# A hybrid transformer layer on one core: two small loads on ScalarE's queue, and a reordered last pair of experts

## The reference, cut to what matters

```python
h = LN(x)                                        # gain ln_in_g, offset ln_in_b
u = h @ w_in                                     # 115 tiles of 128 columns
m = sum_i sigmoid(gate_i) * (branch_i(u) @ wo_i) # gated linear attention, RWKV-7, Mamba-2
h = LN(alpha * h + m @ w_out)
# mixture of experts: 64 experts of width 256, 8 per token, and one shared expert
y = sum_e gate_e * ((silu(h @ w1_e) * (h @ w3_e)) @ w2_e) + shared(h)
out = LN(alpha * h + y)
```

## Time and profile before

| | |
|---|---|
| timed runs (3) | 1514.79, 1517.59, 1517.62 us, median 1517.59 |
| the profiled execution's own time | 1515.74 us |
| its span | 1513.9 us |
| TensorE busy | 1475.3 us, 97% |
| VectorE busy | 644.6 us, 43% |
| ScalarE busy | 389.7 us, 26% |
| GpSimd busy | 112.1 us, 7% |
| moved by the DMA engines | 371.36 MB |

### The profile page before, as it was taken

How to read it: one execution, slowest core, us unless ns; L and a number is a source line. 1 busy time by engine, 2 the same in 40 slices (tenths; PEclk the granted TensorE clock), 3 DMA queues, 4 the chain that set the end, 5 groups by cost and what they waited for, 6 DMA issues and landing times.

```text
span 1513.9 us, 31413 instructions
## 1 busy us (share of the span) xinstructions
PE 1475.3 (97%) x13271; PEld 1046.2 (69%) x13271; DVE 644.6 (43%) x1202; ACT 389.7 (26%) x873; POOL 112.1 (7%) x102
## 2 busy tenths in 40 slices
PE   7999999999999999999999999999999999999995
PEld 6676677777776777677667756777777777777751
DVE  5223787875635777634531133421121121111228
ACT  2112444443223544335421002011111111111111
POOL 4000113122010000000000000000000000000000
PEclk9999999999999999999999999999999999999998
DMA  7777375563345445563677548599999999999965
GB/s 236 166 178 170 111 213 168 135 203 104 108 116 159 112 115 139 193 191 110 195 235 225 148 166 362 195 400 409 417 411 405 415 413 401 418 412 405 411 269 172
DMA packets 155946, 371.36 MB, mean 245 GB/s; under 512 B 101596, under 2 KB 110188, under 8 KB 138144
## 3 DMA queue, kind: packets, MB, share of 16 engines
q1 hardware_dynamic: 123536, 340.11, 64.2%
q10 hardware_dynamic: 26416, 15.41, 3.4%
q0 software_dynamic: 5856, 13.85, 2.7%
HBM read 324.52 MB, written 50.64 MB: 248 GB/s over the span
## 4 chain that ended last, share of the span: by engine, by line
PE 83%; DVE 9%; DMA 2%; DVEq 2%; ACT 1%; issue 1%; ACTq 1%; SPq 0%
PE PS L563 25%; PE PS L1056 14%; PE PS L906 9%; PE PS L1023 8%; PE PS L1075 7%; PE PS L611 3%; DVE region L1455 2%; DVE region L1448 2%; PE PS L1028 2%; PE PS L944 2%; PE PS L1039 1%; ACT L1134 1%; PE PS L1064 1%; PE PS L619 1%; PE PS L804 1%
## 5 line engine op out<-in xcount | busy, mean ns | idle before, releaser
L563 PE MATMUL PS<-h0T,region 128*128 128x320 f32 x1808 | 510.4, 437 | 0.9 <-issue 0.8
L563 PEld LDWEIGHTS PS<-h0T,region 128*128 128x128 f32 x1808 | 336.9, 190 | 144.5 <-issue 12.2
L1134 ACT ACTIVATE region<-PS 128x9 f32<-128x9 f32 (+6 forms) x407 | 148.5, 383 | 686.6 <-PE PS L563 309.8
L1056 PE MATMUL PS<-region 128*64 128x512 f32 x1024 | 229.3, 592 | 0.0
L1056 PEld LDWEIGHTS PS<-region 128*64 128x64 f32 x1024 | 135.9, 137 | 83.3 <-issue 9.1
L1448 DVE TENSOR_TENSOR region<-region 128x256 f32<-128x256 f32 (+10 forms) x210 | 126.3, 621 | 96.1 <-ACTq L1177 75.5
L906 PE MATMUL PS<-region 128*128 128x320 f32 x512 | 138.3, 433 | 1.3 <-DMA region<-wo 1.2
L1023 PEld LDWEIGHTS PS<-region,h 128*128 128x128 f32 x1024 | 119.2, 192 | 26.4 <-issue 26.3
L1023 PE MATMUL PS<-region,h 128*128 128x128 f32 x1024 | 128.1, 278 | 0.3 <-issue 0.3
L906 PEld LDWEIGHTS PS<-region 128*128 128x128 f32 x512 | 97.0, 190 | 42.2 <-issue 1.9
L1075 PE MATMUL PS<-region,history 128*64 128x512 f32 x512 | 120.3, 596 | 0.5 <-ACTq L1413 0.5
(11 more groups left out here) (194 smaller groups left out, 1150.3 us busy)
## 6 DMA issues: line engine op xcount, KB each, us to landing
region<-moe_w SPq DMA_DIRECT2D x64, 2048.0 KB, 12.3
region<-moe_w SPq DMA_DIRECT2D x64, 1024.0 KB, 10.0
region<-w_in SPq DMA_DIRECT2D x115, 512.0 KB, 5.6
region<-wo SPq DMA_DIRECT2D x32, 512.0 KB, 3.8
projected<-region ACTq DMA_DIRECT2D x65, 167.5 KB, 3.9
expert_rows<-region SPq DMA_DIRECT2D x20, 512.0 KB
region<-expert_rows SPq DMA_DIRECT2D x4, 2048.0 KB, 12.6
region<-projected SPq DMA_DIRECT2D x10, 768.0 KB, 6.3
```

Source lines behind the costliest of these rows:

```text
L563: last = mm(PS[:, 6 + i % 2, 0:NTOK], WR[:, i, k, :], H0T[:, k, :], start=(k == 0), stop=(k == KT - 1))
L1056: last = mm(PS[tiles(i), 2, :], XE[:, k, tiles(i)], W13[r][i][:, k * 512:k * 512 + 512], start=(k == 0), stop=(k == KT - 1))
L1134: return nc.scalar.activation(out, in_, f, **kw)
```

## The change

Three things. (1) The loads of `ID` and `GBR` are started by ScalarE, first in its list, and no longer by SyncE between the first and the second token tile. (2) VectorE's list around the last two pairs is changed: the first addition of load 0 (`halve_rows(0)`) is put ahead of `x_step` of the last pair; the first of the two index comparisons is made one pair earlier; the rest of load 0's sum and all of load 1's follow the second comparison; the left copy of `Y` of the pair before last leaves VectorE. (3) ScalarE makes that left copy, behind its right copy and behind the start of one of the two loads of line 529, the one into partitions 64 to 127, which SyncE no longer starts. ScalarE first waits for `rows_out`, so that all scattered rows are in the table.

```diff
+        last_rows = slots[2048:SLOTS, :].rearrange("(p k) d -> p k d", k=8)
-        def sum_rows(e, k):
+        def sum_rows(e, k, halved=False):
             t, w = k // 2, 128 if k < 4 else 64
             rw = ROWS[k][0:w]
-            e.tensor_tensor(rw[:, 0:2], rw[:, 0:2], rw[:, 2:4], ALU.add)
-            e.drain()
+            if not halved:
+                e.tensor_tensor(rw[:, 0:2], rw[:, 0:2], rw[:, 2:4], ALU.add)
+                e.drain()
...
             sp.dma_start(H0[:, 0, :], x[:, 0, :]).then_inc(sem("x_first"), 16)
-            sp.dma_start(ID, io['consts'][:, C_ID:C_ID + 128]).then_inc(sem("ident_in"), 16)
-            sp.dma_start(GBR, io['lnv'][0:2, :].rearrange("r (k f) -> (r k) f", f=128)).then_inc(sem("ident_in"), 16)
             sp.dma_start(H0[:, 1, :], x[:, 1, :]).then_inc(sem("x_rest"), 16)
...
-            rows = slots[2048:SLOTS, :].rearrange("(p k) d -> p k d", k=8)
-            for h in range(2):
-                sp.dma_start(head(ROWS[4], h), rows[:, 4 * h:4 * h + 4, :]).then_inc(sem("halves_in"), 16)
+            sp.dma_start(head(ROWS[4], 0), last_rows[:, 0:4, :]).then_inc(sem("halves_in"), 16)
...
+            act.dma_start(ID, io['consts'][:, C_ID:C_ID + 128]).then_inc(sem("ident_in"), 16)
+            act.dma_start(GBR, io['lnv'][0:2, :].rearrange("r (k f) -> (r k) f", f=128)).then_inc(sem("ident_in"), 16)
...
                 act.wait_ge(sem("rows_out"), n + 1)
                 a_(Y[:, p, 512:D], PS[:, 6, :], ACT.Copy, scale=GA[:, p:p + 1])
                 act.drain().then_inc(sem("y_right"), 1)
+                if isinstance(n, int) and n == NP - 2:
+                    act.wait_ge(sem("rows_out"), SENT + 2)
+                    act.dma_start(head(ROWS[4], 1), last_rows[:, 4:8, :]).then_inc(sem("halves_in"), 16)
+                    a_(Y[:, p, 0:512], PS[:, 5, :], ACT.Copy, scale=GA[:, p:p + 1])
+                    act.drain().then_inc(sem("y_left"), 1)
...
+            def halve_rows(k):
+                dve.wait_ge(sem(f"rows_in{k}"), 16)
+                tt(ROWS[k][:, 0:2], ROWS[k][:, 0:2], ROWS[k][:, 2:4], add)
+                dve.drain()
...
+            def turned_back(p):
+                ts(OH[:, p].rearrange("p a b -> p (a b)")[:, 0:NTOK], CON[:, C_IOTA:C_IOTA + NTOK], TKI[:, p:p + 1],
+                   None, ALU.is_equal)
+                dve.drain().then_inc(sem("turned_back"), 1)
...
             for n in range(NP):
                 hid_step(n)
+                if n == NP - 2:
+                    halve_rows(0)
                 if n + 1 < NP:
                     x_step(n + 1, (n + 1) % 2, n + 1 < SENT)
                 if n + 2 < NP:
                     onehot(n + 2, n % 2, 0)
+                if n == NP - 3:
+                    turned_back(0)
                 if n == NP - 2:
-                    for p in range(2):
-                        ts(OH[:, p].rearrange("p a b -> p (a b)")[:, 0:NTOK], CON[:, C_IOTA:C_IOTA + NTOK], TKI[:, p:p + 1],
-                           None, ALU.is_equal)
-                        dve.drain().then_inc(sem("turned_back"), 1)
-                    add_rows(0)
+                    turned_back(1)
+                    sum_rows(dve, 0, True)
+                    add_rows(1)
                 if n == NP - 1:
                     add_rows(2)
-                y_step(n, n % 2)
-                if n == NP - 2:
-                    add_rows(1)
+                if n != NP - 2:
+                    y_step(n, n % 2)
             add_rows(3)
```

## The result

The changed kernel is slower. Eight runs of it have the median 1522.99 us (1519.95 to 1524.79), eight of the kernel before 1517.51 us; the ratio is 1.0036, 95% interval 1.0026 to 1.0045, which is 4 to 7 us. The forecast was 1516.6 and no measurable change.

A forecast was written before the change was run, and what follows sets the result against it. The wait chain runs over TensorE for 83% of the span, so only its exits at start and end count. Start -0.9 plus end +0.8 gives -0.1 us; from the middle of profiled and median times, 1516.6 us, range 1514.0 to 1519.2.

The forecast's parts named there:

- Step 1: First 14 us: small loads leave SyncE's queue, the second token tile's load is issued earlier; -0.9 us, at most 1.20.
- Step 2: VectorE's list before the last pair: 4.1 us of work gone, last pair's product earlier, 2.2 us won.
- Step 3: Last left copy of Y: at most 0.3 of 2.2 us reach the end, 1.9 become a wait for TensorE.
- Step 4: ScalarE after the pair before last: half load's issue and left copy finish before 1477, nobody waits; price nothing.
- Step 5: Half load on another queue delays load 3's landing to 1490.8; sum of load 3 +0.8 us, ends -0.3 and +2.7.
- R1: Load 3 pushed fully by the upper half load, landing at 1492.7 or 1493; +1.9 us net, 1517.6; chance 0.18.
- R2: Both edits harmless, loads 2 and 3 land in time; end gains 0.3, start 0.9: -1.2 us, 1514.5; chance 0.22.
- R3: Start gives nothing, small loads issued behind ScalarE's table load; start 0 to +0.3, end +0.8: +1.0, 1516.7; chance 0.11.
- R4: All VectorE saving reaches the end, needing the last down product before 1487; -3.1 us, 1512.6; chance 0.04.

The follow-up runs named there:

- the halves on SyncE: The changed kernel with both half loads back on SyncE's queue behind load 3; 1518.24 us, ratio 1.0005 to the kernel before.
- Filling that wait: Changed kernel, last tokens' rows in one wide SyncE load, load 3's first pass ahead of the last left copy of Y; 1514.78 us, ratio 0.9986 to before.
- the wide load on ScalarE's queue: Changed kernel, but ScalarE starts the last tokens' rows as one load over 128 partitions, SyncE only loads 0 to 3; 1518.17 us, one run.

## Why the prediction was wrong

*Step 1, the start.* Size right, reason not borne out. Against the one profile that I read it from, the first projection came 0.77 us earlier where 0.9 were forecast, but that is luck: with the old start it came at 13.18 and 13.26 in two other profiles, with the new one at 13.33 to 13.53 in eleven. The 1.20 us idle before the second tile, which I took for the price of the queue's order, is 0 and 0.18 in those two. What holds is a lead at 139 us, 1.15 us for the changed kernel and 0.3 to 2 us over all pairs of profiles. That it reaches the end is not shown: the tails start up to 4.3 us apart from the kernel before for other reasons.

*Step 2, VectorE's list.* Right: the pass over load 0 starts on its landing, and the product of the last pair comes 17.47 us after the tail's start (1481.23 - 1463.76) against 19.31 (1483.72 - 1464.41), 1.84 us earlier where 2.2 were forecast. Nobody waited for the later token copy.

*Step 3, the gain turns into a wait.* Right, shown with the halves on SyncE: 2.05 us of wait, 1.9 forecast, and 0.17 us left at the end, 0.3 forecast. Filling that wait (1.54 us of tail) shows it was the limit.

*Step 4, ScalarE's new work.* Right: nothing waits for it.

*Step 5, the half load on another queue: this failed.* Forecast +0.8 us with an upper end of +2.7; measured +6.44 at the start of the sum of load 3. Load 2's landing was put at 1484.7 and came at 1484.1. Load 3's was put at 1490.8, at most 1492.7 or 1493, and came at 1495.8. I charged the half load's own 1.05 MB at 209 GB/s, 5.0 us, as the most that it could cost. That price treats only the upper partitions' packets as slow; but the rate of everything fell to 188 to 262 GB/s from 1478 on, lower partitions and all, until the half load was through. The bytes of SyncE's queue show how much that is. Loads 0 to 3 are 8.39 MB; as much had gone through it by 1483.2 in the kernel before (from 1461.5) and by 1490.5 after (from 1461.4):

```profile
q1 hardware_dynamic: 562, 8.37, 93.5%
...
q1 hardware_dynamic: 567, 8.41, 80.8%
```

Counted from load 3's issue (1474.2 and 1473.5) that is 9.0 and 17.0 us, 8.0 us more where I had charged 5.0. The rest of the landing, in which the last packets of load 3 come in while the lower half load moves, was 4.5 us before and 5.3 after. I had put it at 3.6 and reckoned that it would shrink to 1.7, since only one half load is left behind load 3; it did not. The two together, 8.0 and 0.8, are the 8.8 us by which load 3 lands later, 22.3 for 13.5. Which channel lags, and why, is not shown here.

Rival R1 had the mechanism, its place and its sign, and the wrong price, +2.7 to +2.9 for +6.4; I gave it 0.18. The Trainium skill's rule cited there (DMA: Bandwidth & Descriptors, Issuing engines are not separate DMA queues), that transfers from different engines interleave on the same 16 DMA engines, is borne out: the half load on ScalarE's queue and the one ahead in SyncE's cost nearly the same, 6.45 and 5.73 us. What the rule does not price is width, and the wide load on ScalarE's queue cost nothing. R2 (harmless) came true for that wide load only. R3's condition fell, since the small loads were issued ahead of the table load; its outcome at the first projection, nothing gained, is what the two other profiles of the old start show. R4 fell, as its row said.

The bounds were also too tight for another reason: I set them from one resource's arithmetic, where the earlier trace rows had already shown a state in which the whole set of channels ran at half rate. And the times do not stand on one base: the forecast stands on the middle of 1515.74 and 1517.59, the rivals' times on 1515.74 alone, and -2.0 to +2.9 about 1516.6 would reach 1519.5, not 1519.2. The measured 1522.99 lies outside either.

## What to carry to other kernels

Before a transfer is moved ahead of others, look at its partitions: here one load over 64 partitions put 1 MB ahead of a 2 MB load over 128 and delayed it by 7.5 to 8.8 us, while all the rows of both halves, 2 MB spread over 128 partitions, delayed it by 4.7 us, which a wait for TensorE covered. When an in-order engine has spare time in front of a wait, put independent work in front of the wait, since work saved before it only makes the wait longer. Measure a change in a late stage from an event at that stage's start; the executions' own differences further up hide a microsecond or two. And before a wait in one profile is priced, see whether a second profile has it: the 1.20 us at this kernel's start was gone in two others with the same code there.

## What the runs showed of the hardware that was not expected

- A narrow load lowers the rate of the wide loads that move in turn with it from another queue: 188 to 262 GB/s for both together, 418 to 442 without it. Two narrow loads also delay the wide load ahead of them in the same queue by about 2 us.
- Two wide loads in two queues ran at 422 GB/s together. Where load 3 ran at half the rate in a second queue, the first queue was moving the narrow loads.
- After TensorE had stood idle for 4.04 us, its last 16 products in the kernel after took 6.23 us instead of 3.65, with a granted clock of 0.50, the 1.2 GHz level (third column from the right in the row below). They ended at 1504.87, before VectorE came for them at 1505.93, so this cost nothing here.

```profile
1498.00:1500.00 2.00, 1.36 (x4) 0.53 (x6) 1.85 (x3) 0.00 (x0) 0.00 (x0) 0.50 0.00 0
```
